# The last layer's experts in a three-layer transformer kernel: a unit of 64 rows in two column halves, or whole

## The reference, cut to what matters

```python
def swiglu(t, w_gu, w_dn):
    g, u = jnp.split(t @ w_gu, 2, axis=-1)
    return (jax.nn.silu(g) * u) @ w_dn
...
    def one_block(args):
        rb, e = args
        return swiglu(t_pad[rb], w_gu[e], w_dn[e]).astype(jnp.float32)
```

## Time and profile before

| What | us |
| --- | --- |
| Median of 3 runs (4096.61 to 4117.7) | 4097.36 |
| The profiled execution's own time | 4106.68 |
| Its span, first to last instruction | 4104.9 |
| PE busy in the span (share) | 3346.3 (82%) |
| DVE busy | 1311.7 (32%) |
| ACT busy | 774.9 (19%) |
| POOL busy | 725.5 (18%) |
| The last layer's expert stage | about 3343 to 4017 |

### The profile page before, as it was taken

One profiled execution on the slowest core, in us unless ns is written; L12 is line 12 of the kernel. 1 busy time (PEld: TensorE's weight loads), 2 busy tenths in 40 slices (PEclk: granted clock), 3 DMA queues, 4 the chain that ended last, 5 costly groups with the idle time before them and its releaser, 6 DMA issues. The chain is left out here.

```text
span 4104.9 us, 60413 instructions
## 1 busy us (share of the span) xinstructions
PE 3346.3 (82%) x21986; PEld 2035.1 (50%) x21987; DVE 1311.7 (32%) x2475; ACT 774.9 (19%) x1816; POOL 725.5 (18%) x793
## 2 busy tenths in 40 slices
PE   4989989985988868985898866976868779999995
PEld 2559658634544533334554433441534446666662
DVE  2476576524100112123110013027644341111114
ACT  1432343111111111001111111110124112222221
POOL 0015114201111110001111110024200033333334
PEclk7999999995999988996999987988779889999997
DMA  6321021325999983325999983320065349998985
GB/s 253 90 87 42 22 84 37 114 108 206 415 411 408 409 360 115 141 108 218 400 406 414 419 364 130 134 93 0 1 159 121 123 160 366 365 372 315 362 345 197
DMA packets 177898, 910.63 MB, mean 222 GB/s; under 512 B 77096, under 2 KB 79722, under 8 KB 131691
## 3 DMA queue, kind: packets, MB, share of 16 engines
q1 hardware_dynamic: 125516, 782.04, 49.8%
q10 hardware_dynamic: 30628, 76.61, 5.2%
q0 software_dynamic: 21632, 50.37, 3.7%
HBM read 847.37 MB, written 83.59 MB: 227 GB/s over the span
## 5 line engine op out<-in xcount | busy, mean ns | idle before, releaser
L2052 PE MATMUL ps<-moe_spare,moe_xT 128*64 128x128 f32 (+1 forms) x2944 | 521.5, 337 | 0.0
L2189 DVE TENSOR_TENSOR moe_act<-moe_sg,ps 64x128 f32<-64x128 f32 (+1 forms) x328 | 112.8, 344 | 959.6 <-ACT moe_sg L2137 959.6
L2050 PE MATMUL ps<-weight_ring,moe_xT 128*64 128x128 f32 (+1 forms) x2304 | 362.5, 318 | 46.2 <-DMA weight_ring<-in_w_dram 45.1
L2019 POOL COPY moe_xg<-moe_xin 64x1024 f32<-64x1024 f32 x172 | 177.5, 1032 | 1142.1 <-PE ps L2033 865.5
L2052 PEld LDWEIGHTS ps<-moe_spare,moe_xT 128*64 128x64 f32 x2944 | 372.9, 142 | 0.0
L2050 PE MATMUL ps<-moe_spare,moe_xT 128*64 128x128 f32 (+1 forms) x2208 | 344.0, 316 | 33.6 <-issue 33.6
L2052 PE MATMUL ps<-weight_ring,moe_xT 128*64 128x128 f32 (+1 forms) x2304 | 363.0, 318 | 0.0
L2050 PEld LDWEIGHTS ps<-weight_ring,moe_xT 128*64 128x64 f32 x2304 | 283.3, 142 | 154.6 <-issue 62.3
L2050 PEld LDWEIGHTS ps<-moe_spare,moe_xT 128*64 128x64 f32 x2208 | 268.8, 140 | 121.7 <-issue 81.0
L2052 PEld LDWEIGHTS ps<-weight_ring,moe_xT 128*64 128x64 f32 x2304 | 282.3, 142 | 0.0
L2193 DVE COPY moe_y<-ps 128x512 f32<-128x512 f32 x164 | 113.4, 692 | 499.5 <-PE ps L2061 485.3
(11 more groups left out here) (643 smaller groups left out, 5155.8 us busy)
## 6 DMA issues: line engine op xcount, KB each, us to landing
moe_spare<-in_w_dram SPq DMA_DIRECT2D x82, 2048.0 KB, 10.3
weight_ring<-in_w_dram SPq DMA_DIRECT2D x66, 2048.0 KB, 10.7
weight_ring<-in_w_exp_gu_dram SPq DMA_DIRECT2D x32, 2048.0 KB, 10.9
moe_spare<-in_w_exp_gu_dram SPq DMA_DIRECT2D x32, 2048.0 KB, 11.1
moe_y<-in_w_dram SPq DMA_DIRECT2D x22, 2048.0 KB, 10.8
modulation<-in_w_dram SPq DMA_DIRECT2D x22, 2048.0 KB, 11.0
expert_rows<-moe_y ACTq DMA_DIRECT2D x328, 128.0 KB, 8.8
moe_spare<-in_w_exp_dn_dram SPq DMA_DIRECT2D x16, 2048.0 KB, 11.8
```

The costliest lines, as they stand in the source:

```text
L2019: nc.gpsimd.tensor_copy(xg[:], xin[:, b, :]).then_inc(s.x_moved, 1)
L2050: nc.tensor.matmul(m.ps[0:UR, half, 0:W], xT[:, k, :], gate[:, k, cols], start=(k == 0), stop=(k == KD - 1))
L2052: last = nc.tensor.matmul(m.ps[UR:P, half, 0:W], xT[:, k, :], up[:, k, cols], start=(k == 0), stop=(k == KD - 1))
L2189: nc.vector.tensor_tensor(act_[:, cols], sg[UR:P, cols], m.ps[UR:P, half, 0:W], ALU.mult).then_inc(acted[half], 1)
```

## The change

In the last layer (G=2) a unit's columns are no longer halved: NH is 1 there and stays 2 in layers 0 and 1. Gate/up then is one pass over 256 columns, silu, product, activation turns (two pieces in one call), the copy to `moe_aT` and the down product each run once per unit over the whole width, and `moe_aT` is made by one ACT instruction. The order on PE becomes: gate/up, all eight pieces of turn_x, turn_a (two pieces), down product. SP's waits look at the one remaining gate/up semaphore. The amount of arithmetic, the weights, the gathers and the results are the same.

```diff
-    W, CH = F // 2, FC // 2
+    NH = 1 if G == 2 else 2
+    W, CH = F // NH, FC // NH
...
-                        sp.wait_ge(gate_up[1], part)
+                        sp.wait_ge(gate_up[NH - 1], part)
...
-                if half == 1:
+                if half == NH - 1:
                     last.then_inc(s.y_ps, 1)
...
                 pe.wait_ge(acted[0], u + 1)
                 gate_and_up(gate, up, 0, 0, KD)
-                pe.wait_ge(acted[1], u + 1)
-                gate_and_up(gate, up, 1, 0, KD)
-                turn_a(u, 0)
-                turn_x(u + 1, 0)
+                if NH == 2:
+                    pe.wait_ge(acted[1], u + 1)
+                    gate_and_up(gate, up, 1, 0, KD)
+                    turn_a(u, 0)
+                    turn_x(u + 1, 0)
+                else:
+                    turn_x(u + 1, 0)
+                    turn_x(u + 1, 1)
+                    turn_a(u, 0)
                 weights_there(2)
                 pe.wait_ge(s.y_copied, u + 1)
-                down_product(u, down, 0)
-                turn_a(u, 1)
-                turn_x(u + 1, 1)
+                if NH == 2:
+                    down_product(u, down, 0)
+                    turn_a(u, 1)
+                    turn_x(u + 1, 1)
                 after_hi = pe.value_load(r.start[0:1, bass.ds(e + 2, 1)], min_val=0, max_val=r.units)
-                down_product(u, down, 1)
+                down_product(u, down, NH - 1)
                 return after_hi
...
-                gate_silu(u, 0)
-                move_a(u, 0)
-                gate_silu(u, 1)
-                move_a(u, 1)
+                for half in range(NH):
+                    gate_silu(u, half)
+                    move_a(u, half)
                 move_x(u + 1)
...
-                for half in range(2):
+                for half in range(NH):
                     cols = slice(half * W, half * W + W)
                     dve.wait_ge(acted[half], u + 1)
```

More of the change, by code:

```diff
@@ L1970, in load @@
                     elif j == 1 or G == 1:
-                        sp.wait_ge(gate_up[1], last)
+                        sp.wait_ge(gate_up[NH - 1], last)
                     else:
                         part = sp.value_load(r.start[0:1, bass.ds((g - NS_) * G + 1, 1)], min_val=1, max_val=r.units)
-                        sp.wait_ge(gate_up[1], part)
+                        sp.wait_ge(gate_up[NH - 1], part)
                     sp.sem_inc(s.paced, 1)
```

## The result

The changed kernel takes 4154.26 us (median of 4 runs, 4142.56 to 4170.06), the kernel before 4099.16 (4 runs). The ratio is 1.0118, 95% interval 1.0088 to 1.0147: slower by 36 to 60 us. Single runs of one kernel lie up to 28 us apart, so the ratio is the better figure; 1.0118 x 4099.16 is 4147.5.

What follows compares the result with a forecast made beforehand. PE's line of work was taken to set the last layer's pace, DMA close behind. Down's start at 5.55 plus 1.77 gave 7.32 per unit against 6.78; over 96 units, +38.7 us on 4097.4, so 4136, range 4112 to 4150.

Steps and rivals of the forecast that it cites:

- Gate/up, silu, product: Start of a unit: pairs span 3.24 us, silu 0.43 later, product 0.41 after that, ending 4.50 after the unit's start.
- Row turns are free: Between gate/up and activation turns: eight turns start at 3.57 and end about 4.45, before the product's 4.50, costing nothing.
- Turn and move: Product to down: 0.15 to the turn, 0.37 to ACT's move, 0.28 move, 0.05 to 0.14 to down, at 5.35 to 5.44.
- The register read: Sequencer's read before down: ends at 5.45 at the earliest; down's start taken as 5.55, bounds 5.35 to 5.69.
- Down: Unit's last step: four pairs in one go, without the stop in the middle, taking 1.77 us.
- Weights: Waits for down weights: slower PE asks 4.3 us later, so both waits (7.1 us) and their low clock go.
- the 2.6 us of group changes: Stage time left to changes of group and loop; forecast to fall under the longer down product, otherwise 2.6 on top.
- Rival A: Register read hidden under turn and move: 7.12 to 7.21 per unit, +19.5 to +28 us, 4117 to 4125; chance 0.22.
- C: Rival: the 0.49 us per unit of ACT and DVE busy time saved counts in full, 47 us less, 4050; chance 0.03.
- D: Rival: DMA engines carry the last layer's stage, so no measurable change: stage 664 us, time 4097; chance 0.11.
- Rival B: PE's clock falls in the new gap between gate/up and down: 55 us more, 4191; chance 0.03.
- the rule that I had put beside this rival: Trainium skill on HAM oscillation: a kernel's clock fell between matmul bursts each time it waited for data; would give rival B's time.

Runs made afterwards that it cites:

- whole_turns_last: `whole_read_early` with the activation turns put ahead of all eight row turns; ratio 1.0045 to the kernel before, interval 7.17 us per unit.
- halves_turns_first: The kernel before, halves kept, with all eight row turns moved between gate/up and the first activation turn; ratio 1.0084, interval 7.27 us.
- whole_read_early: The changed kernel with the register read moved from ahead of down to right behind gate/up; ratio 1.0042 to the kernel before, interval 7.17 us.
- act_halves_down_whole: The kernel before with early register read and, after halved silu and product, all turns, one move and one down product; ratio 1.0013, interval 6.92 us.
- whole_read_twice: The changed kernel with the register read done twice ahead of the down product; ratio 1.0541 to the kernel before, interval 9.29 us.

## Why the prediction was right, and where it was short

Forecast was +38.7 us on the stage, 4136; the stage gave +47.7. The median of 4154.26 lies 4 us above the upper end of the range, 4150, while 1.0118 times the kernel before, 4147.5, is inside: that the range holds hangs on which of the two one takes. The mechanism is the one forecast; one term was too small, the start of down behind the register read (5.55 taken, 5.65 measured).

- **Gate/up, silu, product.** Right to the hundredth. 3.24 for the pairs, silu 0.43 behind the last (3642.61 to 3643.04), product 0.41 later, ending at 3643.87, which is 4.50 after the unit's start.
- **Row turns are free.** Right: the first stands 3.56 after the unit's start, and all eight end after 0.70, at 4.26 and not at 4.45, since the later ones take 0.07 each and not 0.11. `whole_turns_last` shows that it holds on both sides; `halves_turns_first` shows that it depends on what stands behind them.
- **Turn and move.** 0.15, then 0.34 where 0.37 stood, then 0.28. Behind the move, when nothing else is last, 0.14 (`whole_read_early`); between my 0.05 and 0.14 it was the upper.
- **The register read.** The direction was right, the size short. I took 5.55 for down's start. It is 3644.98 - 3639.37 = 5.61 in the unit shown, and 7.41 - 1.76 = 5.65 in the mean, since with the read last intervals vary from 7.34 to 7.49, while with the read early they stand still at 7.17. My 5.45 "at the earliest" was short in two places. The two more waits that now stand ahead of the read, which I had named, put its first operation at 3644.17, 0.25 behind the wait's release at 3643.92, where it was 0.15 before (3607.24 to 3607.39). And the 5.45 was the time of SEQ_ASSERT, not of the matmul, which comes 0.08 later (3644.90 to 3644.98). The 0.10 that I put on top covered only one of the two. The other 0.1 per unit is the 9 us.
- **Down.** 3644.98 to 3646.74, 1.76 against 1.77.
- **Weights.** Right: no wait for weights is left in the stage, the clock is 1.00 throughout, and the 2.6 us of group changes are gone too: no interval is longer than 7.49, where the kernel before has some of 6.93 to 7.17 among its 6.78, apart from the two stops and the units right behind them.
- **Rival A** (read hidden) fell, and `whole_read_early` is what it would have been: 7.17, inside its 7.12 to 7.21, and a ratio of 1.0042. **C** fell: the 0.49 us of busy time per unit are saved, and the kernel is slower all the same. By the Trainium skill (Perfetto Trace Analysis, Optimizing Scalar/DVE Operations), splitting pays where the engines aren't saturated but cause bubbles; `act_halves_down_whole` against `whole_read_early` shows just that, 6.92 against 7.17 for the same work in two pieces. **D** fell: the stage grew by 47.7 us with no wait for weights in it.
- **Rival B** did not come in, but my reason against it was poor. I compared the longest idle piece with waits elsewhere. In `whole_read_twice` the idle pieces are 0.38 and 1.26 to 1.38, shorter than the 1.61 that had left the clock at 1.00, and it fell. Nor did the rule that I had put beside this rival come in: PE waited in every unit, and the clock stayed at 1.00. But the changed kernel was within 0.75 us per unit of the fall.

Where the 0.63 per unit comes from (6.78 to 7.41): 0.14 for turns, move and down in one piece (6.78 to 6.92; this one is what is left over, not taken apart further), 0.25 for silu and product of full width with nothing beside them (6.92 to 7.17), 0.24 for the register read (7.17 to 7.41). That is 61 us, less the 13.1 us of waits, low clock and group changes that the slower PE no longer meets: 48.

## What to carry to other kernels

Halving a chain of small steps paid here although each half has its own fixed cost: what counts is how much of the chain stands behind the last matmul with nothing to do. When a stop is made longer or moved, list the sequencer's own instructions in front of the next matmul with the same care as the engines' work; a register read of 0.7 us that was hidden became the last releaser, and the profile named another engine for it. Here it paid to take such a read to a place where the sequencer is ahead of the array.

## What the runs showed of the hardware that I had not expected

- PE's clock can fall from gaps that recur though no idle piece in them is longer than 1.4 us, if turns count as work: one more register read of 0.7 us per unit cost 1.9 us per unit (7.42 to 9.29), with a granted clock of 0.87; 16 useless turns in the gap took the interval back to 8.22 and the clock to 0.95. The Trainium skill (TensorE: Matmul & The Clock Gate, A second HAM failure mode) tells of PE idling often for short times between groups of matmuls, and of a clock that swings with it; the trace fits that, but the runs don't tell it from one pause of about 3 us with only turns in it.
- One DMA of 128 partitions in place of two of 64, same bytes, with the memory side in another order: its issue held ACT's sequencer up to 16.2 us, and the kernel got 9% slower.
- Fourteen us taken from PE's line (a mean of 6.82 to 6.67 in the 94 units without a stop) became 8 on the stage, since waits for weights rose from 7.1 to 11.4 us, with low clock behind each.
